# A two-block transformer kernel: the scan's chain step laid over four tiles of the TensorE array, and the depthwise convolution taken in 32x32 diagonals

## The chip, the cores and the metric

The program runs on one core of one Trainium2 chip. The metric is device time in microseconds (us). Five engines work side by side: TensorE (PE, with its weight loads PEld), VectorE (DVE), ScalarE (ACT), GpSimd (POOL) and the queue of SyncE (SP), which here only starts transfers. They meet through semaphores. A TensorE operation multiplies a stationary operand, loaded into the 128x128 array by an LDWEIGHTS, with a moving operand. All data are float32, and each product written in the code becomes two passes, that is two pairs of LDWEIGHTS and MATMUL. A product with 64 or 32 rows and columns uses only a part of the array, a tile; which one follows from the partitions of its operands (rows of the array) and of its output (columns of the array). In what follows (a, b) is the 64x64 tile with row half a and column half b.

## The reference, cut to what matters

The input is a sequence of 256 tokens with 1024 channels. It passes a first block (a hybrid mixer, a conformer convolution, two feed-forward layers) and a second block (an RWKV mixer over 512 tokens, then attention). Two pieces are touched. The conformer's convolution is, for each of 1024 channels, a causal filter of 31 taps:

```python
def causal_depthwise_conv(x, w, b):
    k = w.shape[0]
    out = lax.conv_general_dilated(
        x, w[:, None, :].astype(x.dtype), window_strides=(1,), padding=[(k - 1, 0)],
        dimension_numbers=('NWC', 'WIO', 'NWC'), feature_group_count=x.shape[-1])
    return out + b
```

The RWKV scan carries a 64x64 state per head (16 heads) in each of two directions over 512 tokens:

```python
    def step(s, inp):
        r_t, lw_t, k_t, v_t, a_t, b_t = inp
        sa = jnp.einsum('dbhij,dbhj->dbhi', s, a_t)
        s = s * jnp.exp(lw_t)[..., None, :] + sa[..., None] * b_t[..., None, :] + v_t[..., None] * k_t[..., None, :]
        return s, jnp.einsum('dbhij,dbhj->dbhi', s, r_t)
```

## The kernel before

**Convolution** (`stage_conformer`). Channels lie on partitions: 8 channel tiles of 128, 256 tokens each. A first projection (L306) fills the banks, ACT and DVE gate it into `cv_u`, and then the filter is shared out. DVE takes channel tiles 0 and 1, then 2 and 3, then 4: each tap is one scalar_tensor_tensor over 128x256 (L1237), in a loop that waits for the step before. TensorE takes tiles 5, 6 and 7: POOL builds for every tap a 128x128 diagonal matrix (`cv_diag`, L1179), and TensorE adds up 31 products per channel tile in one bank (L1195, waiting for all eight gated tiles). ACT moves each finished bank out with the bias (L1210). After its part TensorE runs `keep_warm`, products with no use for the result (L139, 16 of them), and the stage ends for all engines at a barrier; the layer norm follows (L1266 is its first product).

**Scan** (`stage_rwkv_scan`). The heads go in 8 slices n of two heads; a head is one half e of the 128 partitions. The 512 tokens are cut into NCK = 16 chunks c of 32. The state of a chunk is the sum of `inner` (L1880: what the chunk adds by itself) and `carried` (L1887: what comes from the chunk before, through `rw_u`); the output is the sum of `read_inner` (L1904) and `read_state` (L1895). DVE scales the new state into `rw_u` (L2282), and the next step of the chain waits for that. One chain step is four such calls, each of four products (direction d = 0, 1; head e = 0, 1). A list (`scan_order`) sets one order for all engines: for each slice it spreads the chain steps evenly over a stretch and fills in between the projections of later slices (L1968, full array, fed by POOL's transfers through six slots of `rw_feed`), the preparation of the next slices (`scan_solve`, `scan_grams`: L1808, L1816, L1826, L1838, L1845, L1861, L1863, L1868) and the readout of the last one. Each engine works through its items in that order.

The two lines that place a chain step's products on the array are these; `rows64(i)` are partitions 64i to 64i+63, and h = c % 2 is the half in which a chunk's operands lie.

```python
mm = pe.matmul(k.psum[h][rows64(e), 64 * d:64 * d + 64], BG[n % 3][d][rows64(h), c2, e, 0:64],
               VQ[n % 2][d][rows64(h), c2, e, :], ...)          # inner: tile (h, e)
mm = pe.matmul(k.psum[c % 2][rows64(e), 64 * d:64 * d + 64], GR[n % 2][d][rows64(e), c, 0:64],
               U[rows64(e), c % 2, d, :], ...)                  # carried: tile (e, e)
```

`read_inner` lies as `inner` does, on (h, e), and `read_state` as `carried`, on (e, e).

## Time and profile before

| | |
|---|---|
| time, median of 3 runs | 2372.62 us (2366.45 to 2377.3) |
| the profiled execution: time, span | 2365.28 us, 2363.6 us |
| mean granted clock of TensorE | 0.965 |
| PE busy | 2173.4 us, 92% of the span |
| DVE, ACT, POOL busy | 43%, 22%, 14% |
| conformer's convolution, from TensorE's first tap to the layer norm | 840.2 to 898.5 us |
| the scan's eight chains | 1435 to 2070 us |

The span runs from the first to the last instruction; the profiled time is 1.7 us longer. Busy shares are means over stages with different limits, and TensorE's share counts the keep-warm products too, so what a change is worth is read from its own stage.

### The profile page before, as it was taken

The page shows a single profiled execution, that of the slowest core. Times are in us where ns is not written, and L with a number is a line of the kernel's source. Part 1 is how long each engine was busy: PE and PEld are TensorE (multiplying, and loading weights), DVE is VectorE, ACT ScalarE, POOL GpSimd, SP SyncE. Part 2 cuts the span into 40 slices and gives each one's busy share as a digit, 9 for nine tenths or more (in the row PEclk, how much of TensorE's full clock was granted, in tenths as well). Part 3 has the DMA queues.
Part 4 walks back from the last instruction along what each step waited for, and adds up shares of the span by engine and source line. Part 5 has one row for each costly group of instructions (what it writes and reads, how often), then busy time and mean ns, then how long its engine had stood idle before and what let it go on. Part 6 is the DMA issues. An engine that isn't in the chain of part 4 may idle for free. (4 is left out here: it accounts for less than half of the span.)

```text
span 2363.6 us, 39368 instructions
## 1 busy us (share of the span) xinstructions
PE 2173.4 (92%) x16594; PEld 1613.0 (68%) x16594; DVE 1015.1 (43%) x2276; ACT 526.0 (22%) x933; POOL 320.4 (14%) x530
## 2 busy tenths in 40 slices
PE   4998999999999998999998889998998899879988
PEld 3887888878888776788853355565566666436656
DVE  4643543524430572578055444534434541140262
ACT  1112122311000101100023243424434431011151
POOL 0000000000000300000005624433432120000100
PEclk8999999999999999999998989999999799899999
DMA  8543347438854320677216746545544252112100
GB/s 358 221 178 143 143 143 209 112 143 318 301 227 162 115 80 36 254 302 295 92 47 246 230 129 163 153 117 143 162 108 119 51 158 83 73 76 107 71 1 18
DMA packets 127130, 359.73 MB, mean 152 GB/s; under 512 B 78696, under 2 KB 87144, under 8 KB 109424
## 3 DMA queue, kind: packets, MB, share of 16 engines
q1 hardware_dynamic: 93776, 209.90, 25.8%
q0 software_dynamic: 32608, 146.31, 18.2%
q8 instruction: 132, 2.16, 0.4%
q10 hardware_dynamic: 576, 1.05, 0.1%
q14 instruction: 38, 0.31, 0.0%
HBM read 340.36 MB, written 16.85 MB: 151 GB/s over the span
## 5 line engine op out<-in xcount | busy, mean ns | idle before, releaser
L306 PE MATMUL bank<-h,ring 128*128 128x256 f32 x2304 | 501.1, 381 | 5.1 <-DVEq L1113 3.3
L306 PEld LDWEIGHTS bank<-h,ring 128*128 128x128 f32 x2304 | 439.2, 191 | 69.5 <-DVEq L1113 4.9
L1968 PE MATMUL bank<-rw_feed 128*128 128x512 f32 x464 | 248.9, 645 | 18.7 <-DMA rw_feed<-in_rkvg 8.1
L1755 POOL DMA_DIRECT2D rw_feed<-rwkv_mixes x232 | 124.8, 538 | 464.5 <-PE bank L1968 456.5
L2282 DVE TENSOR_TENSOR rw_u<-bank,rw_lam 128x128 f32<-128x128 f32 x120 | 34.9, 291 | 294.9 <-PE bank L1887 289.5
L1023 PE MATMUL bank<-ffn_hidden,ring 128*128 128x256 f32 x704 | 152.4, 379 | 3.4 <-PEq L1049 3.4
L1023 PEld LDWEIGHTS bank<-ffn_hidden,ring 128*128 128x128 f32 x704 | 133.6, 190 | 22.2 <-issue 4.1
L527 PE MATMUL bank<-h,ring 128*128 128x256 f32 x640 | 143.1, 380 | 1.1 <-PEq L323 1.1
L1968 PEld LDWEIGHTS bank<-rw_feed 128*128 128x128 f32 x464 | 77.5, 195 | 88.6 <-issue 47.7
L527 PEld LDWEIGHTS bank<-h,ring 128*128 128x128 f32 x640 | 120.2, 190 | 20.2 <-issue 4.8
L139 PE MATMUL bank<-con 128*128 128x512 f32 x220 | 103.2, 621 | 32.3 <-DVE mod L133 14.4
L1756 POOL DMA_DIRECT2D rw_feed<-in_rkvg x232 | 124.5, 537 | 9.8 <-issue 9.8
L133 DVE CUSTOM_DVE_ANT_0 next_w<-next_w,next_vec,par 128x1024 f32<-128x1024 f32 x96 | 120.2, 1280 | 11.4 <-DMA next_w<-in_mod_stream 11.4
L139 PEld LDWEIGHTS bank<-con 128*128 128x128 f32 x220 | 42.5, 196 | 83.0 <-issue 67.7
L1035 DVE SCALAR_TENSOR_TENSOR x<-bank,mod,x 128x256 f32<-128x256 f32 x24 | 10.0, 478 | 176.4 <-PE bank L1023 176.4
L1237 DVE SCALAR_TENSOR_TENSOR cv_v<-cv_u,par,cv_v 128x256 f32<-128x256 f32 x150 | 67.5, 482 | 22.8 <-DVE cv_v L1237 21.7
L1108 ACT ACTIVATE ffn_gate<-bank 128x512 f32<-128x512 f32 x22 | 13.1, 597 | 281.2 <-PE bank L306 281.2
L1887 PEld LDWEIGHTS bank<-rw_u,rw_gr 64*64 64x64 f32 x896 | 36.2, 137 | 56.4 <-issue 53.8
L2464 PE MATMUL bank<-mla_h,ring 128*128 128x256 f32 (+1 forms) x240 | 68.3, 449 | 6.5 <-PEq L231 6.5
L133 DVE CUSTOM_DVE_ANT_0 next_products<-next_w,next_vec,par 128x1024 f32<-128x1024 f32 x48 | 61.4, 1280 | 12.2 <-DMA next_w<-in_mod_stream 12.0
L2464 PEld LDWEIGHTS bank<-mla_h,ring 128*128 128x128 f32 x240 | 47.3, 198 | 28.2 <-issue 23.0
L1895 PE MATMUL bank<-rw_gr,rw_u 64*64 64x32 f32 x960 | 63.7, 222 | 3.0 <-DVE rw_u L2282 3.0
(435 smaller groups left out, 3364.7 us busy)
## 6 DMA issues: line engine op xcount, KB each, us to landing
ring<-in_stream SPq DMA_DIRECT2D x79, 2048.0 KB, 8.1
rw_feed<-rwkv_mixes POOLq DMA_DIRECT2D x232, 256.0 KB, 3.1
next_w<-in_mod_stream POOLq DMA_DIRECT2D x24, 2048.0 KB, 9.9
ctx<-in_mod_rest POOLq DMA_DIRECT2D x16, 1024.0 KB, 6.9
rw_feed<-in_rkvg POOLq DMA_DIRECT2D x232, 64.0 KB, 3.5
y<-bias_table SPq DMA_DIRECT2D x48, 128.0 KB, 4.9
rwkv_mixes<-mixed SPq DMA_DIRECT2D x6, 1024.0 KB, 3.9
rw_at<-rw_at_kept SPq DMA_DIRECT2D x16, 256.0 KB, 4.0
```

The costliest lines, as they stand in the source:

```text
L133: return nc.vector.tensor_tensor_reduce(products, w, vec, 1.0, bias, ALU.mult, ALU.add, out)
L139: pe.matmul(k.psum[bank][:], const(k, "ident"), k.con[:, 0:512], start=True, stop=True)
L306: mm = pe.matmul(out, ring_tile(k, n, kt, i * P), rhs[kt], start=start and kt == kts[0], stop=stop and kt == kts[-1])
L527: mm = pe.matmul(k.psum[6 + pair % 2][:, (t % 2) * T:(t % 2 + 1) * T], ring_tile(k, n, kt, (t % 4) * P), h[:, kt, :], start=(kt == 0), sto ...
L1023: mm = pe.matmul(k.psum[grp * 4 + i][:, 0:T], ring_tile(k, n, kt, i * P), rhs[part * KT + kt], start=(part == 0 and kt == 0), stop=(part = ...
L1237: nc.vector.scalar_tensor_tensor(v[:, i:i + 1, :], u[:, i:i + 1, bass.ds(t * U + j, T)], k.par[:, bass.ds(t * U + (PAR["dw"] + i * (TAPS + ...
L1755: pool.dma_start(feed[:, g % FEED, 0:512], mixes[j, :, g % KT, :]).then_inc(fed[g % FEED], 16)
L1756: pool.dma_start(feed[:, g % FEED, 512:], a["rkvg"][j, n, :, g % KT, :]).then_inc(fed[g % FEED], 16)
L1887: mm = pe.matmul(k.psum[c % 2][rows64(e), 64 * d:64 * d + 64], GR[n % 2][d][rows64(e), c, 0:64], U[rows64(e), c % 2, d, :], start=False, s ...
L1895: mm = pe.matmul(k.psum[2 + c % 2][rows64(e), at:at + 32], U[rows64(e), c % 2, d, :], GR[n % 2][d][rows64(e), c, 64:96], start=(d == 0), s ...
L1968: pe.matmul(k.psum[PROJ], feed[:, g % FEED, 512:], feed[:, g % FEED, 0:512], start=(kt == 0), stop=(kt == KT - 1)).then_inc(eaten, 1)
L2464: mm = pe.matmul(out, ring_tile(k, n, kt, i * P), rhs[kt], start=(kt == 0), stop=(kt == KT - 1))
```

## The change

**Convolution.** TensorE now takes channel tiles 4 to 7, and DVE only 0 to 3. A diagonal is kept as 32 columns: four blocks of 32x32, one for each quarter g of the partitions. Each tap is four products of 32x32, and tap c writes quarter g to output quarter (g + c % 4) % 4, in bank c % 4 of a group of four; so four taps in a row use sixteen different tiles of the array. What stands in the banks is turned by 0 to 3 quarters; ACT copies all four banks at once to `cv_turned`, and four more full-array products with a shifted identity turn and add them. Two small identities are loaded for this at the start of the stage, and the keep-warm products go from 16 to 6.

**Scan.** `read_state` and `read_inner` now write to the other column half (1 - e), so that `carried` with `read_state` uses (0,0), (1,1), (0,1), (1,0), and so does `inner` with `read_inner`, which is taken one chunk later than before (c - 2 instead of c - 1). The calls are interleaved by direction. The chain has one step more (NSTEP = 18 items per slice instead of 17), and the constants and copies behind it follow the exchanged halves.

```diff
-    ON_PE = (5, 6, 7)
+    ON_PE = (4, 5, 6, 7)
+    Q = 32
...
-            diag = ctx.enter_context(nc.sbuf_tensor("cv_diag", [P, len(ON_PE), TAPS, P], F32))
+            diag = ctx.enter_context(nc.sbuf_tensor("cv_diag", [P, len(ON_PE), TAPS, Q], F32))
...
+                def spread_taps(n):
+
+                    i = ON_PE[n]
                     pe.wait_ge(diag_made, n + 1)
+                    if n >= 2:
+                        pe.wait_ge(convolved, n - 1)
                     for c in range(TAPS):
-                        mm = pe.matmul(k.psum[2 * n][:, 0:T], diag[:, n, c, :], u[:, i, c:c + T], start=(c == 0),
-                                       stop=(c == TAPS - 1))
-                    mm.then_inc(convolved, 1)
-                keep_warm(k, pe, 1, 16)
+                        turn = c % 4
+                        for g in range(4):
+                            to = (g + turn) % 4
+                            rows, cols = slice(Q * g, Q * g + Q), slice(Q * to, Q * to + Q)
+                            mm = pe.matmul(k.psum[4 * (n % 2) + turn][cols, 0:T], diag[rows, n, c, :], u[rows, i, c:c + T],
+                                           start=(c < 4), stop=(c >= TAPS - 4), skip_group_check=True)
+                    mm.then_inc(turned_up, 1)
+
+                def combine(n):
+
+                    pe.wait_ge(turned_down, n + 1)
+                    for turn in range(4):
+                        mm = pe.matmul(k.psum[4 * (n % 2)][:, T:2 * T], twice_ident[:, Q * turn:Q * turn + P], turned[:, n % 2, turn, :], start=(turn == 0),
+                                       stop=(turn == 3))
+                    mm.then_inc(combined, 1)
...
+                keep_warm(k, pe, 1, 6)
...
+                for n in range(len(ON_PE)):
+                    act.wait_ge(turned_up, n + 1)
+                    banks = k.banks[:, 2048 * (n % 2):2048 * (n % 2) + 2048].rearrange("p (r t) -> p r t", r=4)
+                    nc.scalar.copy(turned[:, n % 2, :, :], banks[:, :, 0:T]).then_inc(turned_down, 1)
+                    if n:
+                        finish(n - 1)
+                finish(len(ON_PE) - 1)
...
-                done = convolve([2, 3], done)
-                convolve([4], done)
+                convolve([2, 3], done)
...
+NSTEP = NCK + 2
...
+            def read_inner(n, c, d):
+                h, c2, at = c % 2, c // 2, output_column(c, d)
+                for e in range(2):
+                    mm = pe.matmul(output_bank(c)[rows64(1 - e), at:at + LCH], VQ[n % 2][d][rows64(h), c2, e, :],
+                                   BG[n % 3][d][rows64(h), c2, e, 64:96], start=False, stop=True, skip_group_check=True)
                 return mm
...
                 if c < NCK:
                     pe.wait_ge(u_done, (NCK - 1) * n + c)
-                    if c < NCK - 1:
-                        carried(n, c).then_inc(state_up, 1)
+                    for d in range(2):
+                        if c < NCK - 1:
+                            mm = carried(n, c, d)
+                            if d:
+                                mm.then_inc(state_up, 1)
+                        mm = read_state(n, c, d)
+                for d in range(2):
                     if c + 1 < NCK - 1:
-                        inner(n, c + 1)
-                    read_state(n, c)
-                read_inner(n, c - 1).then_inc(step_up, 1)
+                        mm = inner(n, c + 1, d)
+                    if c >= 2:
+                        mm = read_inner(n, c - 2, d)
+                mm.then_inc(step_up, 1)
```

TensorE's instructions in the convolution, as the difference of the two orders (L1218 is a tap's 32x32 products, L1226 the combining ones, L139 keep-warm; each row is one kind of product in the order of the program):

```order
-L1195 MATMUL bank<-cv_u,cv_diag 128x256 x93
-L139 MATMUL bank<-con 128x512 x16
-L1156 UNCONDITIONAL_BRANCH
-L1263 UNCONDITIONAL_BRANCH
-L1266 MATMUL bank<-cv_v,con 128x256 x8
+L1218 MATMUL bank<-cv_u,cv_diag 32x256 x248
+L1226 MATMUL bank<-cv_turned,cv_twice_ident 128x256 x4
+L1218 MATMUL bank<-cv_u,cv_diag 32x256 x124
+L1226 MATMUL bank<-cv_turned,cv_twice_ident 128x256 x4
+L1218 MATMUL bank<-cv_u,cv_diag 32x256 x124
+L1226 MATMUL bank<-cv_turned,cv_twice_ident 128x256 x8
```

The 93 full-array products have become 496 small ones and 16 full ones.

A chain step on TensorE before, between a projection product and the preparation of a later slice (L1887 carried, L1880 inner, L1895 read_state, L1904 read_inner):

```order
515 L1968 MATMUL bank<-rw_feed 128x512
516 L1826 MATMUL bank<-ring,x 32x64 x16
517 L1887 MATMUL bank<-rw_u,rw_gr 64x64 x4
518 L1880 MATMUL bank<-ring 64x64 x4
519 L1895 MATMUL bank<-rw_gr,rw_u 64x32 x4
520 L1904 MATMUL bank<-ring 64x32 x4
521 L1816 MATMUL bank<-con,ring 128x128 x4
```

A chain step of the changed kernel (L1942 carried, L1950 read_state, L1936 inner, L1958 read_inner, L2032 the projection):

```order
466 L2032 MATMUL bank<-rw_feed 128x512
467 L1942 MATMUL bank<-rw_u,rw_gr 64x64 x2
468 L1950 MATMUL bank<-rw_gr,rw_u 64x32 x2
469 L1942 MATMUL bank<-rw_u,rw_gr 64x64 x2
470 L1950 MATMUL bank<-rw_gr,rw_u 64x32 x2
471 L1936 MATMUL bank<-ring 64x64 x2
472 L1958 MATMUL bank<-ring 64x32 x2
473 L1936 MATMUL bank<-ring 64x64 x2
474 L1958 MATMUL bank<-ring 64x32 x2
475 L1842 MATMUL bank<-lora,rw_w 128x512 x2
```

The sixteen products are the same in number; only their order and tiles are new. The end of a slice's chain before:

```order
658 L1895 MATMUL bank<-rw_gr,rw_u 64x32 x4
659 L1904 MATMUL bank<-ring 64x32 x4
660 L1968 MATMUL bank<-rw_feed 128x512 x2
661 L1904 MATMUL bank<-ring 64x32 x4
662 L1968 MATMUL bank<-rw_feed 128x512 x2
663 L1816 MATMUL bank<-con,rw_xa 128x128 x4
```

And the end of a slice's chain after:

```order
549 L1950 MATMUL bank<-rw_gr,rw_u 64x32 x4
550 L1958 MATMUL bank<-ring 64x32 x4
551 L2032 MATMUL bank<-rw_feed 128x512 x3
552 L1958 MATMUL bank<-ring 64x32 x4
553 L2032 MATMUL bank<-rw_feed 128x512 x2
554 L1958 MATMUL bank<-ring 64x32 x4
555 L2032 MATMUL bank<-rw_feed 128x512 x2
```

One small group of four products more stands by itself between full-array products.

## Rows read from the trace of the kernel before

**Rows 1.** The page: busy time of TensorE, and its packets of code.

```profile
PE 2173.4 (92%) x16594; PEld 1613.0 (68%) x16594; DVE 1015.1 (43%) x2276; ACT 526.0 (22%) x933; POOL 320.4 (14%) x530
...
q8 instruction: 132, 2.16, 0.4%
```

**Rows 2.** Timeline of the convolution: start, us, engine, group, idle before.

```profile
840.17 5.20 PE L1195 MATMUL bank<-cv_u,cv_diag 128*128 128x256 f32 x23 [2.17 <-issue]
...
874.60 0.88 DVE L1237 SCALAR_TENSOR_TENSOR cv_v<-cv_u,par,cv_v 128x256 f32<-128x256 f32 x2 [0.18 <-DVE cv_v L1237]
875.69 0.41 DVE L1229 TENSOR_SCALAR cv_v<-cv_u,par 128x256 f32<-128x256 f32 x1 [0.21 <-DVE cv_v L1237]
...
880.41 13.90 PE L139 MATMUL bank<-con 128*128 128x512 f32 x32
880.61 0.47 ACT L1210 ACTIVATE cv_v<-bank,par 128x256 f32<-128x256 f32 x1 [12.91 <-PE bank L1195]
...
897.53 0.48 DVE L1237 SCALAR_TENSOR_TENSOR cv_v<-cv_u,par,cv_v 128x256 f32<-128x256 f32 x1 [0.18 <-DVE cv_v L1237]
898.52 6.75 PE L1266 MATMUL bank<-cv_v,con 128*128 128x256 f32 x16 [4.21 <-PEq L1156]
```

**Rows 3.** Single lines: duration ns min/median/max, first and last start.

```profile
L1195 PE MATMUL bank<-cv_u,cv_diag x186: 377/378/454, 840.2 to 880.2; 128*128 128x256 f32 x186
...
L1179 POOL TENSOR_TENSOR cv_diag<-con,par x3: 6811/6813/6813, 782.8 to 796.4; 128x3968 f32<-128x3968 f32 x3
...
L1895 PE MATMUL bank<-rw_gr,rw_u x960: 192/219/312, 1440.7 to 2067.7; 64*64 64x32 f32 x192
...
L1887 PE MATMUL bank<-rw_u,rw_gr x896: 213/218/366, 1440.3 to 2063.8; 64*64 64x64 f32 x180
L2282 DVE TENSOR_TENSOR rw_u<-bank,rw_lam x120: 279/291/294, 1436.8 to 2064.0; 128x128 f32<-128x128 f32 x120
```

**Rows 4.** Timeline of one chain step on PE (some rows between left out).

```profile
1593.92 1.12 PE L1968 MATMUL bank<-rw_feed 128*128 128x512 f32 x2
1594.98 0.38 PE L1887 MATMUL bank<-rw_u,rw_gr 64*64 64x64 f32 x5
...
1595.67 0.43 PE L1904 MATMUL bank<-ring 64*64 64x32 f32 x7
1596.02 1.98 PE L1968 MATMUL bank<-rw_feed 128*128 128x512 f32 x4
```

**Rows 5.** Timeline of PE: other runs of small products in the scan.

```profile
1435.03 0.47 PE L1880 MATMUL bank<-ring 64*64 64x64 f32 x16
...
1439.25 1.08 PE L1826 MATMUL bank<-ring 32*32 32x64 f32 x32 [0.68 <-ACT ring L2126]
...
1449.65 1.16 PE L1808 MATMUL bank<-rw_xa,ring 64*64 64x64 f32 x64
...
1588.00 0.89 PE L1868 MATMUL bank<-ctx,ring 32*64 32x96 f32 x32
```

**Rows 6.** Busy time by engine in stretches of the scan, clock, DMA.

```profile
1580.00:1660.00 80.00, 73.80 (x1091) 47.71 (x1091) 34.66 (x96) 28.72 (x51) 29.75 (x56) 0.98 0.52 139
...
1420.00:2060.00 640.00, 590.16 (x8789) 387.32 (x8788) 254.61 (x734) 217.52 (x381) 177.34 (x334) 0.95 0.44 122
```

**Rows 7.** Waits: who for whom, us, times, longest.

```profile
DVE rw_u L2282 <- PE bank L1887: 289.5, 90, 8.8
...
PE bank L1808 <- DVE rw_xa L2215: 15.4, 8, 5.2
...
PE bank L1968 <- DMA rw_feed<-in_rkvg: 4.4, 3, 2.8
```

**Rows 8.** Single microseconds of the scan, columns as in the group before last.

```profile
1850.00:1851.00 1.00, 1.00 (x38) 0.76 (x33) 0.40 (x2) 0.00 (x0) 0.54 (x1) 1.00 0.00 0
...
1853.00:1854.00 1.00, 1.00 (x5) 0.36 (x3) 0.65 (x1) 0.00 (x0) 0.00 (x0) 0.81 0.00 0
1854.00:1855.00 1.00, 1.00 (x6) 0.21 (x6) 0.90 (x5) 0.00 (x0) 0.00 (x0) 0.50 0.00 0
```

**Rows 9.** Timeline of ACT: two passes over 128x1024.

```profile
769.58 2.00 ACT L245 ACTIVATE norm_sq_mix<-x 128x1024 f32<-128x1024 f32 x2 [79.79 <-PEq L292]
```

More of the change, by code:

```diff
@@ L1170, in _ @@
             def _(sp):
+                sp.dma_start(small_ident[:], a["small_ident"]).then_inc(idents_landed, 16)
+                for half in range(2):
+                    sp.dma_start(twice_ident[:, half * P:half * P + P], a["con"][:, CON["ident"]:CON["ident"] + P]).then_inc(
+                        idents_landed, 16)
                 load_ahead(k, sp, first, NS)
@@ L1539, in has @@
             return x if 0 <= n < KT else []
-        order += interleave((0, 1, has(i, [("chain", i, c) for c in range(NCK + 1)])),
+        order += interleave((0, 1, has(i, [("chain", i, c) for c in range(NSTEP)])),
                             (0, 0.7, has(i + 1, scan_solve(i + 1))),
@@ L1737, in _ @@
                     k.slot_landed[(first + n) % RING], 16)
[L1738 removed]
+            sp.wait_ge(step_up, NSTEP * KT)
             sp.wait_ge(bon_up, KT)
@@ L1873, in steps_made, with state_rows, output_bank, output_column @@
                     free(gr_down, 4 * u + 2 * half + h + 1, "gr", n, d, half, h)
-            def inner(n, c):
+            def state_rows(c):
+                return k.psum[c % 2]
+            def output_bank(c):
+                return k.psum[2 + c // 2 % 2]
+            def output_column(c, d):
+                return 256 * d + LCH * (2 * (c // 4) + c % 2)
+            def inner(n, c, d):
                 h, c2 = c % 2, c // 2
-                for d in range(2):
-                    for e in range(2):
-                        mm = pe.matmul(k.psum[h][rows64(e), 64 * d:64 * d + 64], BG[n % 3][d][rows64(h), c2, e, 0:64],
-                                       VQ[n % 2][d][rows64(h), c2, e, :], start=(d == 0), stop=(c == 0), skip_group_check=True)
-                return mm
@@ L1884, in carried @@
-            def carried(n, c):
-                for d in range(2):
-                    for e in range(2):
-                        mm = pe.matmul(k.psum[c % 2][rows64(e), 64 * d:64 * d + 64], GR[n % 2][d][rows64(e), c, 0:64],
-                                       U[rows64(e), c % 2, d, :], start=False, stop=True, skip_group_check=True)
-                return mm
-            def read_state(n, c):
-                for d in range(2):
-                    at = 256 * d + 32 * (c // 2)
-                    for e in range(2):
-                        mm = pe.matmul(k.psum[2 + c % 2][rows64(e), at:at + 32], U[rows64(e), c % 2, d, :],
-                                       GR[n % 2][d][rows64(e), c, 64:96], start=(d == 0), stop=False, skip_group_check=True)
-                return mm
@@ L1899, in read_inner @@
-            def read_inner(n, c):
-                h, c2 = c % 2, c // 2
-                for d in range(2):
-                    at = 256 * d + 32 * c2
-                    for e in range(2):
-                        mm = pe.matmul(k.psum[2 + h][rows64(e), at:at + 32], VQ[n % 2][d][rows64(h), c2, e, :],
-                                       BG[n % 3][d][rows64(h), c2, e, 64:96], start=(c == 0 and d == 0), stop=True,
-                                       skip_group_check=True)
+                for e in range(2):
+                    mm = pe.matmul(state_rows(c)[rows64(e), 64 * d:64 * d + 64], BG[n % 3][d][rows64(h), c2, e, 0:64],
+                                   VQ[n % 2][d][rows64(h), c2, e, :], start=(d == 0), stop=(c == 0), skip_group_check=True)
@@ new lines, in inner, with carried, read_state @@
+                return mm
+            def carried(n, c, d):
+                for e in range(2):
+                    mm = pe.matmul(state_rows(c)[rows64(e), 64 * d:64 * d + 64], GR[n % 2][d][rows64(e), c, 0:64],
+                                   U[rows64(e), c % 2, d, :], start=False, stop=True, skip_group_check=True)
+                return mm
+            def read_state(n, c, d):
+                at = output_column(c, d)
+                for e in range(2):
+                    mm = pe.matmul(output_bank(c)[rows64(1 - e), at:at + LCH], U[rows64(e), c % 2, d, :],
+                                   GR[n % 2][d][rows64(e), c, 64:96], start=(d == 0 and c in (1, 2)), stop=False,
+                                   skip_group_check=True)
+                return mm
@@ L2195, in _ @@
             v.tensor_scalar(omka, kas, -1.0, 1.0, ALU.mult, ALU.add)
-            v.scalar_tensor_tensor(cen, headones, -1.0 / 64, ident, ALU.mult, ALU.add).then_inc(inits, 1)
+            for half in range(2):
+                ins = v.scalar_tensor_tensor(cen[:, rows64(half)], headones[:, rows64(1 - half)], -1.0 / 64,
+                                             ident[:, rows64(1 - half)], ALU.mult, ALU.add)
+            ins.then_inc(inits, 1)
             dve.wait_ge(k.tables_landed, 64)
@@ L2957, in constants @@
     out["bias_onehot"], out["bias_neg"] = onehot, negs
+    out["small_ident"] = (p % 32 == np.arange(32)[None, :]).astype(f32)
     s32, col = p % 32, np.arange(64)[None, :]
```

66 lines of the change are left out of this document (42 added, 24 removed).

## The prediction

> **What bounds the kernel now.** I read the page first: TensorE is busy for 92% of the span [rows 1], so a change that shortens TensorE's work can be worth its full size, but only where TensorE is what the stage waits for. So I went on to the timeline of each stage that is touched.
>
> In the convolution it is not. TensorE starts its taps at 840.17 and ACT moves the last of its tiles out from 880.61 to 881.08; TensorE then runs keep-warm products for 13.9 us. DVE begins its fifth channel tile at 875.69 and ends it at 897.53 + 0.48 = 898.01, and half a microsecond behind that the layer norm starts, at 898.52 [rows 2]. The reader is to see that DVE's tile 4 sets the end.
>
> In the scan TensorE does set the pace. Of the 640 us from 1420 to 2060 it is busy 590.2, DVE 254.6, ACT 217.5 [rows 6]. The waits say the same from the other side: DVE waits 289.5 us for `carried` before it can make `rw_u`, in 90 of 120 cases, while TensorE's longest list of waits is 15.4 us for DVE's `rw_xa` and 4.4 us for a feed transfer [rows 3, 7].
>
> **The scan, worked out.** A full chain step is 16 products, 32 pairs. One starts at 1594.98; its last product ends at 1595.67 + 0.43 = 1596.10 and started 0.22 earlier, at 1595.88. That is 0.90 us for 31 distances, 29 ns each [rows 3, 4]. Where do they lie? `carried` and `read_state` go to (e, e), `inner` and `read_inner` to (h, e) with the same h, so one of the four tiles gets 16 of the 32 pairs, two get 8, and one none. 0.90 us over 16 is 56 ns per pair on the fullest tile, for 64 and for 32 moving columns alike.
>
> The gram products (L1808) go round all four tiles: 64 pairs in 1.16 us, less the 0.22 of the last, over 63: 15 ns, or 60 ns per tile. L1826, on two tiles, gives (1.08 - 0.23)/31 = 27 ns, 55 per tile. L1868, four tiles and 96 moving columns, 21 ns, 83 per tile [rows 5]. So tiles run side by side, each at 55 to 60 ns a pair for up to 64 columns, and what counts is the fullest tile.
>
> Pairs on the fullest tile, per slice. Before: step 0 has 4, steps 1 to 13 have 16 each, step 14 has 12, step 15 has 8, step 16 has 4: 236, at 56 ns 13.2 us. After: step 0 has 4; steps 1 to 15 have 8 (in 2 to 13 all four tiles are evenly full); steps 16 and 17 have 4 each: 132, at the 60 ns of the gram products 7.9 us. The extra item costs a change to small tiles and back: the two passes from 1593.92 at 0.43 us (13.90/32) end at 1594.78 and the step starts at 1594.98, 0.20; behind it 1595.88 to 1596.02 is 0.14; together 0.34 us [rows 2, 4]. Per slice 13.2 - 7.9 - 0.34 = 4.9 us, for eight slices 39.5 us.
>
> Not all of it arrives. In 30 of the 120 cases DVE did not wait for TensorE when it made `rw_u` [rows 3, 7]; there DVE is the later one, and a faster step only lengthens TensorE's wait for DVE. I take a quarter off: 30 us. Bounds: 39.5 if all arrives (the more so since DVE waits 289.5 us in sum and would only wait less), 12 if DVE, ACT and the feed turn late as soon as TensorE gains (TensorE's idle time there is 640 - 590 = 50 us already, and it would grow by 27). DVE's signal `state_up` now comes behind six products (12 pairs at 15 ns, 0.18 us) instead of four (8 at 29 ns, 0.23 us), so it is not later. No transfer is added in the scan, and the read-out copies have the same sizes, so I cost these at nothing.
>
> At this place the Trainium skill speaks against the change. By "TensorE: Matmul & The Clock Gate" (Part 1, Wait — 56ns, not 53.3ns?) matmuls never start closer than about 25 ns, however small. The gram row contradicts it, with 64 pairs at 15 ns, and the row decides; it is kept as a rival below.
>
> **The convolution, worked out.** DVE loses tile 4: its last step for tiles 2 and 3 ends at 874.60 + 0.88 = 875.48, which is 22.5 us before 898.01 [rows 2]. That is the gain, if TensorE and ACT are done by then. TensorE has 4 x 31 x 4 = 496 products, 992 pairs. A full-array pair of 256 columns takes 40.0/185 = 216 ns [rows 3]; sixteen tiles side by side would give 13.5 ns, so the 15 ns of the gram products, the closest spacing in the trace, is my value: 14.9 us. The 16 combining products are 32 passes at 216 ns, 6.9 us. ACT's copy of 128x1024 takes 1.0 us [rows 9]; the last of them, and twice the wait for ACT's 0.47 us pass before banks are used again, add some 2.5 us. So TensorE's real work ends at 840.2 + 14.9 + 6.9 + 2.5 = 864.5, and six keep-warm products (12 x 0.43 = 5.2) at 869.7: 5.8 us before DVE. The cover holds up to 20.9 ns per pair. Nearest rows for the other bound: 27 ns, as if only eight tiles ran at once, puts the end at 881.6 and leaves 16.4; 54 ns, one tile per row group (216/4), puts it at 908.4, a loss of 10.4. No row has more than four tiles in use, so both stay in the range.
>
> POOL's diagonals shrink from 3 x 3968 to 4 x 992 columns, at 6.81 us per 3968 some 7 us instead of 20, ready before 800 even if the small transfers of the identities take a few us; TensorE asks at 840 [rows 3]. Code loading: TensorE's 2 x 16,594 instructions came in 132 packets, 251 to a packet, and 0.4% of 16 times the span is 151 us, 1.15 us a packet [rows 1]. 125 pairs at 15 ns take 1.9 us, so loading stays hidden, with 0.7 us to spare per packet; were it 2.5 us, 8 packets would make 20 us, still under the cover.
>
> The layer norm already starts on a cooled array (16 passes in 6.75 us, 0.42 each against 0.216), after 4.21 us of idle time [rows 2, 3]. After the change TensorE idles 6.3 us there, so that stays.
>
> **Sum.** 22.5 + 30 = 52.5 us off the profiled execution's 2365.3: 2312.8. That execution lies 7.3 us under the median of the runs; on the median, 2320.
>
> **Rivals.**
> - *Scan absorbed.* Other engines turn late and 12 of 39.5 us arrive: 2372.6 - 34.5 = 2338. For it: TensorE already waits 5.2 us at once for DVE [rows 7]. Against: 80 us stretches with DVE busy for 34.7 only [rows 6].
> - *Convolution at the low clock.* The clock falls during small products. In the scan it fell to 0.5 after 1853, out of a stretch in which TensorE was busy in every microsecond, at small products [rows 8]. At 1.2 GHz passes double: 26.8 + 13.8 + 2.5 + 10.3 from 840.2 ends at 893.6, gain 4.4: 2338. Against: in the 80 us from 1580 the same kind of products ran at a mean of 0.98 [rows 6], and the row shows only that it fell once, not for which of them.
> - *The 25 ns floor of the rule.* 480 pairs per slice make 12.0 instead of 13.2 us, less 0.34, eight times 0.9 is 7, of which 5 arrive; the convolution ends at 879.6, gain 18.4: 2349.
> - *Slower:* the small tiles of the convolution do not run side by side, since up to four row groups send to the same columns at once, which no row shows. With two streams only, 108 ns per pair, it ends at 962, 64 later than before, less the scan's 30: 2407. It decides from 74 ns per pair, where (0.992 x 74 + 14.6 + 840.2) is 30 us behind 898.
>
> **How the numbers follow.** The forecast as summed has 0.68, with its own range of 2306 to 2334. Scan absorbed 0.12, low clock or 27 to 54 ns 0.10, the rule 0.04, slower 0.04; 0.02 for what I don't see. The range of 2300 to 2346 takes in the forecast with all of the 39.5 us and some cooled stretches shortened, and the first two rivals. A measurement tells about 0.5%, 12 us, from no change. Faster by more 0.92, within 0.04, slower 0.04.
>
> **What the profile of the changed kernel would show.** In the convolution: L1218 pairs 15 ns apart, DVE's last step at about 875.5, the layer norm's first product half a microsecond later, and TensorE idle before it for some 6 us at a clock of 1.0 until then. In the scan: a full step 0.47 us from first to last start, tiles evenly full; DVE's wait for `carried` down by less than 40 us; TensorE's waits for `rw_xa` up by some 10. Wrong would be: L1218 spaced over 21 ns, the granted clock at 0.5 between 840 and 875, or steps that are 0.47 long while the distance between steps is as before.

## The result, and the profile after

The changed kernel took 2331.18 us (median of 4 runs, 2329.06 to 2348.82) against 2369.53 us for the kernel before, measured beside it (4 runs, 2365.24 to 2377.3): ratio 0.9854, interval 0.982 to 0.9888. The forecast was 2320, range 2300 to 2346. Measured again later, the same kernel gave a median of 2362.04 (7 runs, 2337.86 to 2374.64), which is outside that range, against 2369.66 for the kernel before: ratio 0.9914 [0.9865, 0.9963]. So it is faster by 1.5% in one measurement and by 0.9% in the other, by less than forecast, and its 11 runs scatter over 46 us where 56 runs of the kernel before scatter over 29. Both facts need a cause. (A ratio is not the quotient of the medians, and leaves out a run more than 1.5% above the fastest of its kernel, which is one of the seven here and one of e7's nine; medians, ranges and means keep it.)

The profiled execution took 2329.94 us, span 2328.1 (before: 2363.6), mean granted clock 0.965, as before. Its page:

```profile
PE 2112.6 (91%) x17412; PEld 1546.9 (66%) x17412; DVE 995.9 (43%) x2246; ACT 530.3 (23%) x938; POOL 306.6 (13%) x531
...
q8 instruction: 139, 2.28, 0.4%
```

TensorE lost 60.8 us of busy time [rows 1]; the span lost 35.5. The stage from the first product of the conformer's first projection (781.38) to the first product of its last (905.00) is 17.1 us shorter, and the rest of the gain, 17.3 us, came between that projection and the end. The stage first. Timeline of TensorE and the last rows of DVE and ACT, to be held against [rows 2]:

```profile
838.39 4.55 PE L1218 MATMUL bank<-cv_u,cv_diag 32*32 32x256 f32 x215 [1.52 <-issue]
846.00 6.42 PE L1218 MATMUL bank<-cv_u,cv_diag 32*32 32x256 f32 x256 [3.06 <-issue]
852.91 0.70 PE L1218 MATMUL bank<-cv_u,cv_diag 32*32 32x256 f32 x25 [0.49 <-issue]
853.54 1.99 PE L1226 MATMUL bank<-cv_turned,cv_twice_ident 128*128 128x256 f32 x8
856.19 2.10 PE L1218 MATMUL bank<-cv_u,cv_diag 32*32 32x256 f32 x95 [0.66 <-ACT cv_v L1249]
859.77 2.74 PE L1218 MATMUL bank<-cv_u,cv_diag 32*32 32x256 f32 x128 [1.49 <-issue]
863.23 0.70 PE L1218 MATMUL bank<-cv_u,cv_diag 32*32 32x256 f32 x25 [0.71 <-issue]
...
872.82 0.88 DVE L1284 SCALAR_TENSOR_TENSOR cv_v<-cv_u,par,cv_v 128x256 f32<-128x256 f32 x2 [0.18 <-DVE cv_v L1284]
...
874.17 3.72 PE L1226 MATMUL bank<-cv_turned,cv_twice_ident 128*128 128x256 f32 x16
877.73 5.31 PE L139 MATMUL bank<-con 128*128 128x512 f32 x12
877.93 0.47 ACT L1249 ACTIVATE cv_v<-bank,par 128x256 f32<-128x256 f32 x1 [1.25 <-PE bank L1226]
883.34 3.69 PE L1312 MATMUL bank<-cv_v,con 128*128 128x256 f32 x16 [0.30 <-PEq L1157]
```

DVE is done at 873.70 (forecast 875.48; the stage had begun 1.1 us earlier). But the last of the taps' 992 pairs starts at 873.9, and the keep-warm products end at 883.04, 0.30 us ahead of the layer norm: TensorE itself now ends the stage. The taps do not stand close. After a first run of 215 pairs they come in lots of 128: the run of 256 is two of them, and 25 pairs, 8 combining ones and 95 pairs make one too. Between the lots lie pauses of 0.49 to 3.06 us, and no engine is named behind them, only "issue". Grouped by line, from 838 to 876 (busy us, mean ns, then idle time and its releasers):

```profile
L1218 PE MATMUL bank<-cv_u,cv_diag 32*32 32x256 f32 x992 | 22.8, 405 | 10.8 <-issue 9.4 <-ACT cv_v L1249 1.3
```

One chain step of the scan on TensorE (compare [rows 4]):

```profile
1562.06 0.27 PE L1942 MATMUL bank<-rw_u,rw_gr 64*64 64x64 f32 x2
...
1562.53 0.23 PE L1936 MATMUL bank<-ring 64*64 64x64 f32 x2
1562.69 2.84 PE L2032 MATMUL bank<-rw_feed 128*128 128x512 f32 x6
```

The 32 pairs take 0.48 us from first to last start (forecast 0.47) and 0.63 to the next full-array product. So the step is as short as it was meant to be. Over the whole scan, two windows placed alike, from 15.6 us before the first `rw_u` to 0.4 before the last; before:

```profile
1421.20:2063.60 642.40, 592.56 (x8825) 388.83 (x8826) 255.68 (x737) 217.20 (x380) 176.89 (x334) 0.95 0.43 122
```

and after:

```profile
1400.00:2025.00 625.00, 551.04 (x8817) 341.47 (x8816) 256.27 (x737) 217.05 (x380) 176.44 (x334) 0.95 0.44 125
```

TensorE's busy time fell by 41.5 us, its idle time rose from 49.8 to 74.0 (by 24.1), and the stretch is 17.4 shorter. In which waits the idle time lies is in the waits of the same window (us, times, longest), the first two of TensorE's:

```profile
PE bank L1855 <- DVE rw_xa L2282: 21.9, 9, 8.7
PE bank L2038 <- DVE ring L2335: 9.2, 6, 1.5
```

The first was 15.4, longest 5.2 [rows 7]; the second was 0.8. DVE's own wait for `carried`, 289.5 us in 90 cases before, is now, from 1420 to 2060:

```profile
DVE rw_u L2349 <- PE bank L1942: 247.0, 84, 8.6
```

### The profile page after: what moved, and what is told of

It is laid out like the page before. It is cut to its first block and busy times, and to the rows that moved or that the text cites. A ratio compares the mean times of both kernels' runs of the same rounds, so it can differ in the third digit from the quotient of the medians.

```text
span 2328.1 us, 40907 instructions
## 1 busy us (share of the span) xinstructions
PE 2112.6 (91%) x17412; PEld 1546.9 (66%) x17412; DVE 995.9 (43%) x2246; ACT 530.3 (23%) x938; POOL 306.6 (13%) x531
## 3 DMA queue, kind: packets, MB, share of 16 engines
q10 hardware_dynamic: 576, 1.05, 0.1%
## 5 line engine op out<-in xcount | busy, mean ns | idle before, releaser
L2032 PE MATMUL bank<-rw_feed 128*128 128x512 f32 x464 | 247.9, 645 | 14.7 <-ACT rkv L2237 5.1
L2032 PEld LDWEIGHTS bank<-rw_feed 128*128 128x128 f32 x464 | 78.3, 195 | 89.4 <-issue 49.7
L139 PE MATMUL bank<-con 128*128 128x512 f32 x200 | 95.1, 626 | 32.1 <-DVE mod L133 14.4
L139 PEld LDWEIGHTS bank<-con 128*128 128x128 f32 x200 | 39.1, 199 | 78.2 <-issue 62.9
L1942 PEld LDWEIGHTS bank<-rw_u,rw_gr 64*64 64x64 f32 x896 | 35.8, 136 | 50.0 <-issue 45.9
L133 DVE CUSTOM_DVE_ANT_0 next_products<-next_w,next_vec,par 128x1024 f32<-128x1024 f32 x48 | 61.4, 1280 | 12.3 <-DMA next_w<-in_mod_stream 12.2
L2297 DVE TENSOR_TENSOR rw_x<-rw_x,rw_outer 128x30 f32<-128x30 f32 (+7 forms) x240 | 59.8, 249 | 8.2
L2295 DVE TENSOR_TENSOR rw_outer<-rw_x,rw_at 128x30 f32<-128x30 f32 (+7 forms) x240 | 58.8, 245 | 6.0
```

Of the source, the lines that this page charges most:

```text
L133: return nc.vector.tensor_tensor_reduce(products, w, vec, 1.0, bias, ALU.mult, ALU.add, out)
L139: pe.matmul(k.psum[bank][:], const(k, "ident"), k.con[:, 0:512], start=True, stop=True)
L1942: mm = pe.matmul(state_rows(c)[rows64(e), 64 * d:64 * d + 64], GR[n % 2][d][rows64(e), c, 0:64], U[rows64(e), c % 2, d, :], start=False, s ...
L2032: pe.matmul(k.psum[PROJ], feed[:, g % FEED, 512:], feed[:, g % FEED, 0:512], start=(kt == 0), stop=(kt == KT - 1)).then_inc(eaten, 1)
L2295: s(v.tensor_tensor(t, Xb[:, 0:m, i:i + 1].to_broadcast([P, m, w]), ATb[:, i:i + 1, i + 1:].to_broadcast([P, m, w]), ALU.mult))
L2297: s(v.tensor_tensor(Xb[:, 0:m, i + 1:], Xb[:, 0:m, i + 1:], t, ALU.add))
```

## The experiments

Each expectation names its own theories. Besides the ratio I read two things of each profile: the length of the scan from the first to the last `rw_u`, and for how much of it the granted clock stood at its lower level, 0.5. Both are in the table behind the experiments.

**The two halves alone.** `e1_conv_only` has the convolution's hunks of the diff and no others, `e2_scan_only` the scan's.

> The convolution part of the change alone; the scan is as before. Between the first product of the conformer's first projection and that of its last one the changed kernel was 17.1 us shorter than before (123.6 against 140.7). If the two parts are independent, this kernel is 17 us faster than before (18 with the 1.1 us by which the changed kernel was ahead already in front of the stage), about 2352 us. If instead the scan's start gained from the other part (the changed kernel was 3 us further ahead at the first rw_u than at the start of the second block), it is nearer 20.

> The scan part alone; the convolution is as before. Independent parts: 17 us faster than before, about 2352 us. My prediction had 30 us for this part; if the measured profile of the changed kernel was an unlucky one, it shows here as 25 or more.

Measured: e1 2357.35 us, ratio 0.994 [0.9915, 0.9966]; e2 2361.44, 0.9962 [0.9931, 0.9993] (10 runs each, 19 of the kernel before). Both medians miss the 2352 that independent parts were to give. The convolution's stage in e1 is 124.88 us long, 15.9 less than before, near the 17.1 expected. In e2's profile the scan is longer than before, 636.35 us against 627.23, with 122.9 us of low clock in it against 61.4, although each step is the short one (this is the slowest of e2's ten runs; the others reach down to 2345.73). So the scan's gain is there and something takes it away again, which only the clock column shows.

**Taps of a quarter of the columns.** `e3_few_columns` leaves out three quarters of each tap's columns:

```diff
-  mm = pe.matmul(k.psum[4 * (n % 2) + turn][cols, 0:T], diag[rows, n, c, :], u[rows, i, c:c + T],
+  mm = pe.matmul(k.psum[4 * (n % 2) + turn][cols, 0:64], diag[rows, n, c, :], u[rows, i, c:c + 64],
```

> The changed kernel, but each of the convolution's 32x32 products moves only 64 of the 256 columns (three quarters of the tokens of channel tiles 4 to 7 are left out). Same number of instructions. Theory A (code loading): the pauses behind every 128 pairs come from the loading of code, so the time per 128 pairs stays near 3.46 us and the stretch from the first to the last small product stays near 35 us. Theory B (the array or its banks set the pace, the pauses are the array's): a quarter of the columns makes the pairs at least twice as fast, and the stretch falls to 20 us or less.

Measured: one run, 2336.98 us. Timeline of TensorE:

```profile
837.48 2.32 PE L1218 MATMUL bank<-cv_u,cv_diag 32*32 32x64 f32 x215 [1.52 <-issue]
844.22 1.95 PE L1218 MATMUL bank<-cv_u,cv_diag 32*32 32x64 f32 x128 [4.42 <-issue]
848.77 1.95 PE L1218 MATMUL bank<-cv_u,cv_diag 32*32 32x64 f32 x128 [2.60 <-issue]
...
861.23 1.95 PE L1218 MATMUL bank<-cv_u,cv_diag 32*32 32x64 f32 x128 [2.08 <-issue]
864.96 0.50 PE L1218 MATMUL bank<-cv_u,cv_diag 32*32 32x64 f32 x25 [1.77 <-issue]
```

The runs are shorter and the pauses longer by as much: from 861.23 to 864.96 it is 3.73 us for 128 pairs, where the changed kernel has 3.46 (859.77 to 863.23). That is no effect of the columns, for e1, with all of them, has lots of 4.28, 4.00, 3.73 and 3.46 us, and e3 of 4.55, 4.00 and 3.73. The taps end later, not earlier. What sets the distance is not the array but how fast instructions come: a packet of code holds about the 256 instructions of 128 pairs (2 x 17,412 in 139 packets is 250 each), and the runs break off by just that number. The granted clock fell to 0.50 at 841.9 here, two microseconds into the first pause, and came back at 869.2.

The trace also holds the packets of queue 8, which carry the code. Those around the pauses of the changed kernel, in us:

| pause of TensorE | packet begins | packet lands | from landing to the next product |
|---|---|---|---|
| 842.57 to 846.00 | 843.68 | 844.65 | 1.35 |
| 857.91 to 859.77 | 857.09 | 858.19 | 1.58 |
| 862.14 to 863.23 | 861.00 | 861.95 | 1.28 |
| 868.24 to 870.08 | 867.46 | 868.58 | 1.50 |
| 872.45 to 873.53 | 871.21 | 872.14 | 1.39 |

(A pause here runs from the start of the last product to that of the next one.) A packet takes 1.0 to 1.1 us by itself. But it begins only when the lot before it is under way (859.77 to 861.00 and 870.08 to 871.21, 1.1 to 1.2 us into it), and its products start 1.3 to 1.6 us after it has landed. The three parts add up to the 3.46 us of a lot, whatever the array needs for it.

**The same convolution in 64x64 diagonals.** `e7_conv_64` halves the number of pairs, at twice the length of each:

```diff
-    Q = 32
+    Q = 64
...
-                        turn = c % 4
-                        for g in range(4):
-                            to = (g + turn) % 4
+                        turn = c % 2
+                        for g in range(2):
+                            to = (g + turn) % 2
```

> The changed kernel with the convolution by 64x64 diagonals: four tiles of the array instead of sixteen, two turns instead of four, so 496 pairs instead of 992 and half as many combining products. Theory A (code loading): four tiles at 216 ns each give 54 ns per pair, 128 pairs take 6.9 us, far above the time of loading a packet, so no pauses: 26.8 us of small products, 3.5 us of combining, some 2.5 us of waits; TensorE is through with its part some 33 us after its start instead of 39.3, and keep-warm ends at 838.4 + 33 + 5.2 = 876.6 instead of 883.0: 6 us faster than the changed kernel. Theory B (array): the same 54 ns per pair but then sixteen tiles should have had no pauses either, and its 35 us would be due to the array: this run would be no faster.

Measured: 2342.84 us, 0.9868 [0.9834, 0.9901]. Timeline of TensorE:

```profile
839.90 14.04 PE L1218 MATMUL bank<-cv_u,cv_diag 64*64 64x256 f32 x248 [1.52 <-issue]
...
873.39 5.31 PE L139 MATMUL bank<-con 128*128 128x512 f32 x12
879.00 3.69 PE L1312 MATMUL bank<-cv_v,con 128*128 128x256 f32 x16 [0.30 <-PEq L1157]
```

248 pairs in one run without a pause, (14.04 - 0.4)/247 = 55 ns each, four tiles side by side (216/4 = 54). The stage is 117.77 us long, 5.9 less than with 32x32 (6 expected), with more work for the array: 128 pairs take 7.1 us here, twice the 3.46 us that loading needs, and it keeps up.

**No keep-warm products.** `e8_no_keep_warm` is the changed kernel without this line; `e10_conv64_no_warm` is e7 without it:

```diff
-                keep_warm(k, pe, 1, 6)
```

> The changed kernel without the six keep-warm products behind the convolution. ACT's last pass ended at 878.4 and the six products at 883.0, so the layer norm can start 4.6 us earlier, with TensorE idle for about 1 us only. If the keep-warm products set the stage's end, it is 4 to 5 us faster than the changed kernel; if the clock falls without them, the layer norm's products take twice as long and the gain is 0 to 1 us.

> The changed kernel with both edits on the convolution: 64x64 diagonals and no keep-warm products. The first alone shortened the stretch from the first projection to the last by 5.9 us, the second by 6.1. Together DVE becomes the end of the stage (its last tap at 874 to 875 in all profiles), so the stretch should be 112 to 113 us against 123.6 of the changed kernel, and the whole 11 us (0.5%) faster. If DVE were not the next bound, it would be up to 12; if the clock falls in TensorE's idle time of some 2 us, 8.

Measured: e8 2343.42, 0.9882 [0.9834, 0.993]; e10 2334.79, 0.9847 [0.9812, 0.9882]. The layer norm of e8:

```profile
878.01 3.69 PE L1311 MATMUL bank<-cv_v,con 128*128 128x256 f32 x16 [0.82 <-PEq L1157]
```

It starts 5.3 us earlier than in the changed kernel and its 16 passes still take 3.69 us, not 6.75 as before [rows 2]: TensorE's pause ahead of it is 0.82 us and no longer 4.21. The stage is 117.50 us in e8, 6.1 less (4 to 5 expected), and 114.51 in e10, 9.1 less (112 to 113 us expected). In e10 DVE's last tap ends at 874.91 and the layer norm starts at 875.42: DVE sets the end of the stage again, as the change had meant it to.

**The step with the old tiles.** `e4_old_tiles` keeps the new order and the one chunk later of `inner`, and takes the exchange of halves back:

```diff
-  mm = pe.matmul(output_bank(c)[rows64(1 - e), at:at + LCH], U[rows64(e), c % 2, d, :],
+  mm = pe.matmul(output_bank(c)[rows64(e), at:at + LCH], U[rows64(e), c % 2, d, :],
```

> The changed kernel, but the scan's reads write to the column half of their own head again, as before the change; order of calls, number of steps and banks are those of the changed kernel. Theory of the fullest tile: in a full step the fullest tiles hold 12 of the 32 pairs (16 before the change, 8 after), so first to last start is 12 x 56 = 0.67 us (0.90 before, 0.48 after) and the step takes 0.82 us to the next full-array product. If it is the interleaved order and not the tiles, it stays at 0.48; if it is the tiles of each pair of calls, it goes back to 0.90. The whole would be some 5 to 15 us slower than the changed kernel, since 94 steps lose 0.2 us each and part of it falls where TensorE waits anyway.

Measured: one run, 2361.54 us. A step:

```profile
1562.84 0.33 PE L1942 MATMUL bank<-rw_u,rw_gr 64*64 64x64 f32 x4
...
1563.53 0.22 PE L1936 MATMUL bank<-ring 64*64 64x64 f32 x1
1563.58 0.65 PE L1908 MATMUL bank<-con 64*64 64x256 f32 x4
```

0.70 us from first to last start, between the 0.48 of the full change and the 0.90 of before. With 12 of the 32 pairs on its fullest tile, 12 x 56 ns is 0.67. So the time of a step goes by its fullest tile.

The same run tells where the idle time of the scan comes from. Its window, placed as above, and one of its waits there:

```profile
1404.00:2056.70 652.70, 586.96 (x8819) 373.33 (x8820) 256.55 (x737) 217.56 (x380) 177.12 (x334) 0.93 0.43 120
PE bank L2038 <- DVE ring L2335: 8.6, 6, 1.4
```

TensorE is idle for 65.7 us, where it was 49.8 before the change and 74.0 with all of it, and the wait for the bonus operand is 8.6 of the 9.2 us already. So most of the added idle time comes in with the new order and the eighteenth item per slice, and not with the shorter steps. This is one profile, and its own steps are 0.2 us shorter than before; order and item are not separated.

**DVE relieved.** `e5_before_less_dve` and `e6_after_less_dve` leave out 29 of the 31 steps in which DVE inverts the triangular blocks of a slice, e5 in the kernel before, e6 in the changed one:

```diff
+                if 1 < i < LCH - 1:
+                    return
```

> The kernel before, but DVE leaves out the triangular solve of the scan except its first and last step (58 of DVE's operations per slice, some 15 us of it), so the output is not the reference's. It is the partner of the next run. TensorE's waits for DVE shrink; I expect it 5 to 15 us faster than the kernel before.

> The changed kernel with the same part of DVE's work left out. Theory D (DVE is late at the end and start of each slice and takes back what TensorE gains): with DVE relieved the scan part brings nearly its full 40 us, so this run is 50 us or more faster than its partner, against 35.5 between the two original kernels. Theory P (ping-pong: the gain goes into latencies between engines, ACT and the preparation's own chain, whatever DVE's load): the distance stays at 35 to 40 us.

Measured, one run each: 2355.54 and 2298.5 us, 57.0 apart where the full kernels' profiled runs are 35.3 apart. By itself that meets the 50 us of theory D. Windows placed as above, of e5:

```profile
1412.50:2051.80 639.30, 595.91 (x8822) 389.48 (x8822) 165.80 (x363) 216.78 (x379) 175.72 (x332) 0.95 0.44 122
```

and of e6:

```profile
1389.70:1996.30 606.60, 541.81 (x8850) 335.21 (x8843) 165.81 (x363) 217.81 (x382) 176.92 (x334) 0.97 0.46 129
```

DVE has 90 us less to do in both, yet TensorE's idle time still rises by 21.4 us from e5 to e6 (43.4 to 64.8), nearly as much as with DVE loaded (24.1). The gain of the scan is 32.7 against 17.4, but e6 has 31 us less of low clock in its scan than e5, and by the price worked out below (0.37 to 0.44) that is 11 to 14 of the 15.3. So DVE's load costs some 2 to 4 us of the scan's gain, if the clock of these single runs is chance; the waits themselves stayed (16.9 us for the grams' operand, 9.2 for the bonus's). That speaks against the account by which DVE is simply too slow. Where a piece stands in DVE's list is the other account, and the next experiment's.

**The operands earlier.** `e11_earlier_elements` is e10 with another order of DVE's work: the gram operands of a slice and the bonus operand are made ahead of their old places.

```diff
-            ("exps", n, 0)]
+            ("exps", n, 0), ("el", n, 0)]
...
+                            (0.24, 0.3, has(i + 2, [("rk", i + 2, 0)])),
                             (0.3, 0.36, has(i + 2, [("bonus", i + 2, j) for j in range(2)])),
```

> As the run before, and in the scan DVE's work is moved ahead of TensorE's: the first of a slice's two element stages stands at the end of the stretch before instead of at the start of its own, the product for the bonus stands 6% of a slice ahead of TensorE's use of it, and the triangular solve ends at 0.94 instead of 1. Nothing is left out. Theory D (DVE late at the seams of the slices takes back some 25 us of the gain): TensorE's waits for rw_xa and for the bonus fall from 22 + 9 us to under 15 together, and the scan is 10 to 20 us shorter than in the run before, at the same time at the low clock. Theory P (ping-pong of latencies): the waits move to other names and the scan stays within 5 us.

Measured: 2325.07 us, 0.9816 [0.9785, 0.9848], the best of the kernels that leave nothing out. TensorE's wait for the bonus operand is gone from its list, and the one for the grams is 12.6 us from 1420 to 2060, longest 5.1 (21.6, longest 8.7 in the changed kernel). The scan is 26.3 us shorter than e10's, of which 34 us less of low clock make 13 to 15, so some 12 are the order's, within theory D's 10 to 20. But the first `rw_u` comes 8.4 us later: most of that work has only moved ahead of the scan, and by run and clock (below) the order alone is worth no more than 1 to 2 us against e10.

**Spare products ahead of the waits.** `e12_warm_waits` is the changed kernel with full-array products, whose results nobody reads, ahead of the two waits of TensorE for DVE:

```diff
+  if n >= 3:
+      for _ in range({(6, 0): 3, (7, 0): 8}.get((n, d), 1)):
+          pe.matmul(outs[0].rearrange("p (a b) -> p a b", a=4), ident,
+                    ident.unsqueeze(1).to_broadcast([P, 4, P]), start=True, stop=True)
   pe.wait_ge(el_done, u + 1)
```

and one such product ahead of `pe.wait_ge(rk_done, n + 1)`. `e9_after_again` is the changed kernel itself, measured again.

> The changed kernel once more, as a partner on the same chip for the next two. In the profiles so far the same scan took 609.9 us from its first to its last rw_u in one run with 61 us of it at the low clock, and 632.4 in another (without keep-warm) with 123 us at the low clock. So I expect 2330 to 2345 us, and if its scan is slow again, that its share at the low clock is larger too, by about 0.37 us of time for each us at the low clock.

> The changed kernel, with full-array products of no use put in front of TensorE's waits for DVE in the scan: one ahead of each bonus product and ahead of the gram products from slice 3 on, three and eight ahead of the two longest waits (3.7 and 8.2 to 8.7 us in the profiles of the changed kernel, in front of the gram products of slices 6 and 7). Each takes 0.86 us, and they fit the idle times seen (1.5, 1.7, 3.7, 8.7 us). The changed kernel had from 61 to 133 us of its scan at the low clock in different runs, with 0.37 us of time for each. Theory C (idle waits let the clock fall, and the further waits behind it keep it down): less than 61 us at the low clock, the scan at 600 to 610 us, and times within 2320 to 2345 instead of 2338 to 2375, at a ratio to the kernel before of 0.985 or less. Theory I (it is the kind of products, or a fall that has nothing to do with the waits): the share at the low clock stays at 61 to 133 us, and the ratio at 0.99 or above.

Measured: e9 2362.04, 0.9914 [0.9865, 0.9963]; e12 2334.85 (4 runs, 2333.15 to 2340.44), 0.9866 [0.9844, 0.9888] on its own 7 runs of the kernel before. The scan's second half, 1800 to 2030, in e9:

```profile
1800.00:2030.00 230.00, 200.46 (x3107) 128.30 (x3105) 75.74 (x230) 62.32 (x111) 28.62 (x54) 0.81 0.33 100
```

in the changed kernel's first profile:

```profile
1800.00:2030.00 230.00, 193.46 (x3251) 120.92 (x3249) 80.62 (x246) 60.77 (x106) 26.50 (x50) 0.93 0.30 95
```

and in e12:

```profile
1800.00:2030.00 230.00, 206.98 (x3416) 128.85 (x3416) 81.25 (x247) 63.61 (x113) 27.93 (x53) 0.94 0.32 99
```

The same program ran this stretch at a mean of 0.93 once and 0.81 once. Over the scan's window e9 is 27.5 us longer than the first profile, with TensorE busy for 33.3 us more and idle for 5.8 less: the 27 us went into slower products, and no wait explains them. For e12, theory C had named less than 61 us of low clock, a scan of 600 to 610 us and times from 2320 to 2345, and all three came (48, 608.1, up to 2340.44); its ratio of 0.985 or less was just missed.

**The table.** The scan from first to last `rw_u`, and the low clock in it, one profiled execution each; then the mean of the granted clock and of the time over all runs of the kernel, and what that time would be at a clock of 0.963 (the mean of before) at 20.5 us per 0.01, the slope over the 56 runs of before.

| kernel | scan us | low clock us | runs | mean clock | mean us | at 0.963 |
|---|---|---|---|---|---|---|
| before | 627.2 | 61 | 56 | 0.9631 | 2370.5 | 2370.6 |
| after and e9 | 609.9; 637.3 | 61; 133 | 11 | 0.9562 | 2349.1 | 2335.1 |
| e1 convolution only | 637.0 | 79 | 10 | 0.9625 | 2357.9 | 2356.8 |
| e2 scan only | 636.4 | 123 | 10 | 0.9574 | 2362.8 | 2351.3 |
| e7 64x64 | 616.3 | 79 | 9 | 0.9576 | 2340.0 | 2328.8 |
| e8 no keep-warm | 632.4 | 123 | 10 | 0.9561 | 2344.2 | 2330.1 |
| e10 64x64, none | 624.9 | 96 | 6 | 0.9583 | 2335.3 | 2325.7 |
| e11 earlier operands | 598.6 | 61 | 6 | 0.9620 | 2326.2 | 2324.2 |
| e12 spare products | 608.1 | 48 | 4 | 0.9663 | 2335.8 | 2342.5 |

Two readings. Down the scan column, all with the same steps: 609.9 at 61 us of low clock, 616.3 at 79, 624.9 at 96, 632.4 and 636.4 at 123, 637.3 at 133: 0.37 to 0.44 us for each us at 0.5. The scan of before scatters too: e1, whose scan is the same, took 9.8 us longer at 17 us more, so a pair of single profiles is good to some 3 us. And across: with the clock taken out, the convolution is worth 13.8 us, the scan 19.3, both together 35.5, and the runs of the changed kernel lose 14 us of it to a lower clock (0.9562 against 0.9631). The slope is of different runs on several chips, so these are good to a few us. The kernels with the short steps and neither e11's order nor e12's spare products, e2 and e7 to e10 among them, all lie between 0.956 and 0.959; before and e1, with the old steps and the old order, at 0.963. (e4's one run, old tiles in the new order, had 0.956.)

## Why the prediction was right, and where its sizes were off

The forecast held in sign and, in the first measurement, in range: the time is 11 us over it. Some of this is luck. The second measurement lies outside the range, and the median of all 11 runs, 2347.75, just outside. The gain was 38 us in the first measurement, for 52.5 forecast. Step by step:

**The step by its fullest tile: right.** 0.48 us for 0.47 forecast, and e4's 0.70 for the fullest tile of 12 pairs. The pairs of a step stand 15.4 ns apart, and those of e3's first run, of 215, at some 10 ns, (2.32 - 0.2)/214. With these the rival of the 25 ns floor is out. The Trainium skill ("TensorE: Matmul & The Clock Gate", Part 1, "Wait — 56ns, not 53.3ns?") gives that floor; the traces show pairs at well under it, and they decide.

**The sum of the steps: right.** TensorE's busy time in the scan's window fell by 41.5 us at the same 61 us of low clock, for 39.5 summed. A full step went from 1.05 us up to the next other product to 0.63 (medians). The shorter groups follow their fullest tile as well: 24 pairs, with 8 on it, take 0.47 us from first to last start.

**"I take a quarter off: 30 us": too little.** At the same 61 us of low clock the scan gained 17.4 us. TensorE was busy 41.5 us less, so nothing was wrong with the work removed; 24.1 us of it turned into idle time. My 12 to 39.5 held it, and the idle time of 27 that I named with the lower bound is nearly what came. DVE's wait for `carried` fell by 42.5 us, a little more than the 40 I had named as the most. Two DVE operands account for 15 of the 24, the grams' (+6.5) and the bonus's (+8.4); 10.2 of the 17.4 us were gained in the first four slices. My argument that DVE "would only wait less" looked at `rw_u` alone, where DVE waits for TensorE, and left out what DVE makes for a later slice in the gaps between. It also put the new order at nothing beyond the 0.34 us of the added item, and e4 has 15.9 of the 24.1 us, the bonus's 8 among them, with the old tiles. The rival "scan absorbed" is so half true: its mechanism, not its size. Why DVE's relief (e5, e6) hardly mends it and e11's order takes away the waits without shortening the kernel by as much is open; the time moves to other waits.

**"Loading stays hidden, with 0.7 us to spare per packet": the step that failed.** I took 1.15 us a packet from the page's share of queue 8 [rows 1], and a packet does take 1.0 to 1.1 us by itself. What I left out is that it begins 1.1 us into the lot before and is used 1.3 to 1.6 us after it lands: 3.46 us from one packet's first pair to the next one's, no less in e3, where the array needs far less, and no pause in e7, where 128 pairs take 7.1 us. Eight packets at 3.46 us make 27.7, 7.0 more than the 20.7 that the cover of 20.9 ns a pair holds. That is 27 ns a pair, the value of the nearest bound, though not for its reason of eight tiles at once. And it is beyond 21 ns, my own sign that this part is wrong. The array alone would have stayed under the cover: the pairs of the run of 128 stand (2.74 - 0.37)/127 = 18.7 ns apart and those of the first run 19.5, more than the 15 I took but less than 20.9. So more than four tiles work side by side (216/18.7 is 11.6), and the slower rival is out.

**The convolution: 17.1 of 22.5.** TensorE was to end its keep-warm products at 869.7 and ended them at 883.0. 5.8 us of that was covered, so the layer norm began at 883.34 and not at 876.0; the stage had begun 1.1 us earlier, which makes 8.4 us lost. 3.1 came back, against my step "so that stays": with TensorE busy up to 0.30 us before it, the layer norm ran at a clock of 1.0. 22.5 - 8.4 + 3.1 = 17.2. The rival with the low clock in the taps came only in part: the clock fell in the first pause, for 3.4 us from 845.4, and its mean from 838 to 876 is 0.96, with 0.91 in e8 and 0.60 in e3. The lots of this run kept their 3.46 us through it.

**What I had not costed: the clock of the scan.** I let it stand at 0.95. In the two windows of the first profile it did. Over all runs it fell from 0.9631 to 0.9562, at 20.5 us per 0.01. Between the best run (2329.06 at 0.964) and the worst (2374.64 at 0.946) the clock makes 37 of the 46 us. The kernel's idle time and its share of small products both changed. e12, which puts full-array products where TensorE waited, has the highest mean clock of the table (0.9663) and the narrowest times, which speaks for the waits as part of the cause. It pays for that with its own products: 2342.5 at equal clock. Why the clock fell is not shown, though. e11 also raised it (0.962) by an edit of the order alone, e6's one run had 0.975 with TensorE idle for 64.8 us of its scan, and e12 and e9 were measured at different times with 4 and 7 runs.

## What to carry to other kernels

Cut small products by laying them on all tiles of the array, and count the pairs on the fullest tile; but count instructions too: below some 27 ns a pair (3.46 us by 128) the array waits for code here, so fewer and longer products (64x64, with less use of the array per pair) end earlier. After a stage's slow engine has been relieved, look at what was harmless beside it, here the keep-warm products, which became the end of the stage. And where an edit takes busy time from TensorE in a stage with many short waits, compare the mean granted clock over many runs before believing one profile.

## What the runs showed of the hardware that was not expected

- Code came at 3.46 to 4.55 us for 128 pairs of small products (256 instructions), though the packets take 0.4% of the queues' time on the page. In the changed kernel each took 1.0 to 1.1 us by itself, began about 1.1 us after the lot before had started, and was used 1.3 to 1.6 us after it landed. The Trainium skill ("Runtime: NRT & Kernel Launch", section "Instruction fetch mechanics") has packets of 256 instructions, as here, and their loading hidden behind the issue of instructions; that holds in e7's taps and not in those of the changed kernel.
- Products of 32x32 laid on sixteen tiles, with 256 moving columns, stood 18.7 to 19.5 ns a pair apart in runs of 128 and 215, against 216 ns for a full-array pair. With 64 columns the distance went down to 10 ns in a run of 215 at a clock of 1.0, and to 13 ns in those of 128.
- The same program spent 61 us of its scan at the lower clock in one profile and 133 in another, which made 27 us, in busy time and not in waits.
